# One stage for the modulation columns and the first projection of a two-block transformer layer

## The reference, cut to what matters

```
sh1, sc1, gt1, sh2, sc2, gt2 = split(silu(c) @ w_ada + b_ada, 6)              # w_ada is 2048 x 12288
csh1, csc1, ...              = split(silu(c_ctx) @ w_ada + b_ada, 6)
h  = rmsnorm(x,   norm1_g) * (1 + sc1)  + sh1
ch = rmsnorm(ctx, norm1_g) * (1 + csc1) + csh1
rq, rk, rv, rg, mq, mk, mv, mo, mg, gr, gm = split(h @ w_in)                  # and the same of ch
```

## Time and profile before

| | |
|---|---|
| median of three executions | 3499.36 us (3496.66 to 3500.38) |
| profiled execution, first to last instruction | 3498.0 us |
| mean granted TensorE clock | 0.914 of full speed |
| last matmul of phase 2 begins | 428.75 us |
| PE / PEld / DVE / ACT / POOL busy over the span | 84 / 59 / 53 / 33 / 68% |
| moved by DMA | 1015.86 MB, mean 290 GB/s |

### The profile page before, as it was taken

How to read it: one execution, slowest core, us unless ns; L and a number is a source line. 1 busy time by engine, 2 the same in 40 slices (tenths; PEclk the granted TensorE clock), 3 DMA queues, 4 the chain that set the end, 5 groups by cost and what they waited for, 6 DMA issues and landing times. The chain is left out here.

```text
span 3498.0 us, 31036 instructions
## 1 busy us (share of the span) xinstructions
PE 2928.4 (84%) x11330; PEld 2066.9 (59%) x11330; DVE 1862.3 (53%) x2379; ACT 1143.5 (33%) x1853; POOL 2390.3 (68%) x1133
## 2 busy tenths in 40 slices
PE   5899999999976666665456776569999999999999
PEld 1687778788853333322122232238888888888887
DVE  0767365532457787868888787761137421111121
ACT  2422354454421111111122112124445344444443
POOL 0444675688836676757677666758767688888887
PEclk9999999999988888877777887779999999999999
DMA  9899753455669999999999999986545455666554
GB/s 414 296 346 347 248 165 127 133 193 187 234 263 427 425 427 425 427 425 428 415 427 427 425 427 404 427 336 202 172 155 191 133 181 193 212 204 204 191 188 169
DMA packets 305995, 1015.86 MB, mean 290 GB/s; under 512 B 21916, under 2 KB 26616, under 8 KB 234928
## 3 DMA queue, kind: packets, MB, share of 16 engines
q1 hardware_dynamic: 228870, 472.46, 39.1%
q0 software_dynamic: 73728, 536.90, 36.4%
q10 hardware_dynamic: 3244, 4.51, 0.3%
HBM read 1009.58 MB, written 4.23 MB: 290 GB/s over the span
## 5 line engine op out<-in xcount | busy, mean ns | idle before, releaser
L670 POOL TENSOR_TENSOR block_weights_lo<-weight_ring,block_weights_hi 128x1024 fp32r<-128x1024 f32 x608 | 1483.6, 2449 | 611.1 <-ACT block_weights_hi L663 498.6
L1764 PE MATMUL banks<-up_rows,pick_diagonal 128*128 128x512 f32 x1024 | 675.4, 821 | 469.4 <-DMA up_rows<-peer_up,picked_experts 403.1
L663 ACT ACTIVATE block_weights_hi<-weight_ring 128x1024 fp32r<-128x1024 f32 x608 | 641.2, 1059 | 976.0 <-PE banks L2831 315.8
L1764 PEld LDWEIGHTS banks<-up_rows,pick_diagonal 128*128 128x128 f32 x1024 | 261.8, 268 | 852.2 <-issue 745.6
L1670 POOL DMA_INDIRECT up_rows<-peer_up,picked_experts x256 | 477.4, 1865 | 338.2 <-PE banks L1764 113.4
L2057 DVE CUSTOM_DVE_ANT_0 down_rows<-down_rows,h_tokens 128x2048 f32<-128x2048 f32 x256 | 584.3, 2290 | 203.2 <-DMA down_rows<-peer_down,picked_experts 198.3
L1662 POOL DMA_INDIRECT down_rows<-peer_down,picked_experts x256 | 422.3, 1649 | 116.2 <-issue 79.5
L2017 DVE SCALAR_TENSOR_TENSOR expert_sum<-up_rows,pick_share,expert_sum 128x2048 f32<-128x2048 f32 x125 | 293.9, 2351 | 57.9 <-ACT pick_share L1887 52.7
L1881 ACT ACTIVATE pick_gelu<-pick_dots 128x2 f32<-128x2 f32 x127 | 25.8, 203 | 828.1 <-DVE pick_dots L2057 828.0
L2264 PE MATMUL banks<-block_weights_hi,h_T_hi 128*128 128x512 f32 x704 | 282.2, 401 | 2.7 <-PEq L1534 2.7
L2266 PE MATMUL banks<-block_weights_hi,h_T_lo 128*128 128x512 f32 x704 | 275.2, 391 | 0.0
(11 more groups left out here) (500 smaller groups left out, 4412.2 us busy)
## 6 DMA issues: line engine op xcount, KB each, us to landing
weight_ring<-w_in SPq DMA_DIRECT2D x232, 1024.0 KB, 5.0
cond_ring<-w_ada SPq DMA_DIRECT2D x128, 512.0 KB, 6.1
weight_ring<-w_ada SPq DMA_DIRECT2D x32, 1024.0 KB, 8.6
weight_ring<-w_out SPq DMA_DIRECT2D x32, 1024.0 KB, 5.0
weight_ring<-peer_query SPq DMA_DIRECT2D x16, 1024.0 KB, 16.3
weight_ring<-w_ret_out SPq DMA_DIRECT2D x8, 1024.0 KB, 4.9
weight_ring<-w_mlstm_out SPq DMA_DIRECT2D x8, 1024.0 KB, 4.9
weight_ring<-w_mem_kv SPq DMA_DIRECT2D x8, 1024.0 KB, 16.4
```

What stands on the lines that cost most here:

```text
L663: act.activation(self.hi[:, self.place(slot, h)], ring.tile[:, slot, h * self.HALF:(h + 1) * self.HALF], ACT.Copy).then_inc(self.hi_ready, 1)
L670: pool.tensor_tensor(self.lo[:, at], ring.tile[:, slot, h * self.HALF:(h + 1) * self.HALF], self.hi[:, at], ALU.subtract).then_inc(ring.us ...
L1764: mm = pe.matmul(ps[:, 4 + b], diag[:, G % 2], up[:, p % ROWS, b * CG:(b + 1) * CG], start=(G % PER_TB == 0), stop=(G % PER_TB == PER_TB - ...
```

## The change

Both phases become one, `phase_opening`, with one set of semaphores and no barrier between them.

- SP issues `x` and `ctx` itself, before all else. The 32 tiles of `w_ada` now hold 128 rows of 1024 shift and 1024 scale columns. Tiles 0 to 15 (stage 0) give shift and scale of row blocks 0 to 7, tiles 16 to 31 (stage 1) those of row blocks 8 to 15. Behind each stage's tiles SP loads two tiles of `w_in`, so that the sequence has 36 entries, i = 0 to 35, over the four ring slots: 16 and 17 are `w_in` tiles 0 and 1, and 34 and 35 are tiles 2 and 3. The quarters are no longer begun before all 32 tiles are used.
- PE transposes two pairs of row blocks after each of `w_ada` tiles 4 to 7, instead of one row block after each of tiles 10 to 25. ACT copies the `x` part and DVE the `ctx` part, 512 columns at a time.
- After the first tile of stage 1, PE turns the columns of stage 0; ACT and DVE then modulate row blocks 0 to 7. From tile 20 on, PE runs one piece of the dense products of `w_in` tiles 0 and 1 after each tile of `w_ada`: 12 of their 16 pieces. The other 4 follow after the last tile.
- DVE does all modulation before its first quarter, and `QUARTERS` changes.
- Small tensors of phase 1 lie where the ring of the quarters will be.

The core of the diff (bodies that moved without a change of their instructions are left out):

```diff
-        QUARTERS = (8, 10, 10, 10, 10, 10, 6, 0)
+        QUARTERS = (2, 12, 12, 12, 11, 11, 4, 0)
+        STAGES, PAIRS = 2, KB // 2
+        STAGE_K, STAGE_W = KB // STAGES, SLOTS // STAGES
+        ADA_TILES = STAGES * KB
+        OPENING = STAGES * (KB + STAGE_W)
+        X_FROM, X_PER = 4, 2
+        PIECES_FROM = 4
+        is_weight = lambda i: i % (KB + STAGE_W) >= KB
+        weight_of = lambda i: i // (KB + STAGE_W) * STAGE_W + i % (KB + STAGE_W) - KB
+        base = ring.turn + OPENING // SLOTS - 1
         @block.sync
+            sp.dma_start(e.x[:], tokens_of(io["x"][0])).then_inc(x_in, 16)
+            sp.dma_start(raw, tokens_of(io["ctx"][0])).then_inc(ctx_in, 16)
+            for i in range(OPENING):
+                s, k = divmod(i, KB + STAGE_W)
+                before, slot = i - SLOTS, i % SLOTS
+                if before >= 0 and is_weight(before):
+                    sp.wait_ge(ring.used, base * SLOTS + weight_of(before) + 1)
+                elif before >= 0:
+                    sp.wait_ge(ada_used, ada_before(before) + 1)
+                if before >= 0:
+                    sp.sem_inc(ring.granted, 1)
+                if is_weight(i):
+                    sp.dma_start(ring.tile[:, slot], k_tile(w_in, weight_of(i), slice(RK, RK + CG))).then_inc(ring.landed[slot], 16)
+                else:
+                    rows = io["w_ada"][0][k * P:(k + 1) * P, 0:2 * D].rearrange("p (a n) -> p a n", a=2)
+                    sp.dma_start(ring.tile[:, slot].rearrange("p (a q) n -> p a (q n)", a=2), rows[:, :, s * 2 * CG:(s + 1) * 2 * CG]).then_inc(ada_landed[slot], 16)
+            sp.wait_ge(ada_used, ADA_TILES)
             for m in range(TILES):
...
         @block.scalar
...
+            for f in range(PAIRS):
+                act.wait_ge(x_turned, f + 1)
+                act.activation(e.hT[:, 2 * f:2 * f + 2].rearrange("p k t -> p (k t)"), ps[:, 4 + f % 2], ACT.Copy).then_inc(x_out, 1)
             act.dma_start(e.gate_bias[:], ...)
             act.dma_start(w_gate, ...)
+            act.wait_ge(ctx_turned_out, PAIRS)
...
             def modulate(first):
+                act.wait_ge(stage_ready, first // STAGE_K + 1)
                 for k in range(first, first + TILE_K, 2):
...
+            split.write_hi(act, ring, (0, base), 0)
             modulate(0)
             for m in range(TILES):
                 split.write_hi(act, ring, ((m + 1) % SLOTS, base + (m + 1) // SLOTS), m + 1)
                 if m + 1 < SLOTS:
                     modulate((m + 1) * TILE_K)
...
         @block.tensor
...
+            opening_pieces = [(m, h, j) for m in range(STAGE_W) for h in range(2) for j in range(2 * TB)]
+            for n in range(ADA_TILES):
+                s, k = divmod(n, KB)
+                ada_tile(s, k)
+                for f in range((n - X_FROM) * X_PER, (n - X_FROM + 1) * X_PER):
+                    if 0 <= f < PAIRS:
+                        if f == 0:
+                            pe.wait_ge(xn_ready, 4)
+                        turn_x(f)
+                if s and k == 0:
+                    turn_stage(s - 1)
+                p = n - KB - PIECES_FROM
+                if p >= 0:
+                    if p == 0:
+                        pe.wait_ge(x_out, PAIRS)
+                        pe.wait_ge(ctx_turned_out, PAIRS)
+                    dense_piece(*opening_pieces[p])
+            turn_stage(STAGES - 1)
+            for p in range(ADA_TILES - KB - PIECES_FROM, len(opening_pieces)):
+                dense_piece(*opening_pieces[p])
+
             for m in range(TILES):
-                dense(m)
+                if m >= STAGE_W:
+                    dense(m)
...
         @block.vector
...
+            for f in range(PAIRS):
+                dve.wait_ge(ctx_turned, f + 1)
+                dve.tensor_copy(e.chT[:, 2 * f:2 * f + 2].rearrange("p k t -> p (k t)"), ps[:, 2 + f % 2]).then_inc(ctx_turned_out, 1)
+            dve.wait_ge(x_out, PAIRS)
+            for s in range(STAGES):
+                dve.wait_ge(ada_used, (s + 1) * KB)
+                dve.tensor_copy(stage_rows[:, s % 2], bank_of(s)).then_inc(stage_out, 1)
+                dve.wait_ge(stage_turned, s + 1)
+                for a in range(2):
+                    step(dve.tensor_tensor(ada_of(s, a), turned_of(s, a), bias_of(s, a), ALU.add))
...
+                dve.wait_ge(stage_ready, s + 1)
+                for first in range(s * STAGE_K, (s + 1) * STAGE_K, TILE_K):
+                    for k in range(first + BY_SCALAR, first + TILE_K):
+                        sum_x(k)
+                    for k in range(first, first + TILE_K, 2):
+                        low_x(k)
+                        low_x(k + 1)
+                        low_ctx(k)
+                        low_ctx(k + 1)
+            for q in range(ADA2 * SLOTS):
```

More of the change, by code:

```diff
@@ L205, in gemm_token_major @@
             mm.then_inc(tb_done, 1)
[L208 to L334, removed]
-                tr.then_inc(cond_turned, 1)
-    ring.turn += ADA1
@@ L339, in phase_projection, with phase_opening @@
[L339 removed]
+def phase_opening(nc, e):
     ring, ps, io = e.ring, e.ps, e.io
@@ L353, in phase_projection @@
         w_gate_hi, w_gate_lo = w_gate_split[:, :, 0], w_gate_split[:, :, 1]
-        w_in, base = io["w_in"][0], ring.turn
+        w_in = io["w_in"][0]
+        cond_at = next_place(nc)
+        cond_tile = sb("cond_ring", [P, 4, TILE_K // 2, CG])
+        early = lambda name, shape, at: nc.alloc_sbuf_tensor_at(name, shape, F32, offset=cond_at + at)
+        raw, xn = e.cxt[:, :, 0:D], e.lat[:, 1, 0:TB * D].rearrange("p (b d) -> p b d", b=TB)
+        TILE_M = 32
+        rows_a, rows_b = early("rows_a", [P, P], 0), early("rows_b", [92, P], 512)
@@ new lines, in phase_opening @@
+        PIECES_FROM = 4
+        assert OPENING % SLOTS == 0 and 4 * TILE_M == P
+        is_weight = lambda i: i % (KB + STAGE_W) >= KB
+        weight_of = lambda i: i // (KB + STAGE_W) * STAGE_W + i % (KB + STAGE_W) - KB
+        ada_before = lambda i: sum(1 for n in range(i) if not is_weight(n))
+        base = ring.turn + OPENING // SLOTS - 1
+        ada_landed = [sem(f"ada_landed{s}") for s in range(SLOTS)]
+        ada_turn = lambda i: sum(1 for n in range(i % SLOTS, i + 1, SLOTS) if not is_weight(n))
@@ new lines, in phase_opening @@
+        assert ring.turn == 0 and all(i % SLOTS == weight_of(i) for i in range(OPENING) if is_weight(i))
+        bank_of = lambda s: ps[:, s % 2]
+        turned_of = lambda s, a: ps[:, 6 + s % 2].rearrange("p (i a q m) -> p a q i m", a=2, q=2, m=TILE_M)[:, a, :, :, 0:2]
+        ada_of = lambda s, a: e.ada[:, a * KB + s * STAGE_K:a * KB + (s + 1) * STAGE_K].rearrange("p (q i) v -> p q i v", q=2)
+        bias_of = lambda s, a: e.cols_a[:, a * KB + s * STAGE_K:a * KB + (s + 1) * STAGE_K].rearrange("p (q i) -> p q i", q=2).unsqueeze(3).to_broadcast([P, 2, TILE_K, 2])
@@ L503, in lhs, with dense_piece @@
                 return e.chT_hi[:, k, cols], e.chT_lo[k][:, cols]
+            def dense_piece(m, h, j):
+                c, t = divmod(m, SLOTS)
+                at, q = split.place(t, h), first_out[c] + j
+                if j == 0 and h == 0:
+                    pe.wait_ge(split.first_ready, m + 1)
+                elif j == 0:
+                    pe.wait_ge(ring.used, (base + c) * SLOTS + t + 1)
+                if c == 0 and j in (0, TB):
+                    pe.wait_ge(x_ready if j == 0 else ctx_ready, t * TILE_K + (h + 1) * split.HALF)
+                if t == 0 and h == 0 and q >= OUT_BANKS:
+                    pe.wait_ge(cols_out, q - OUT_BANKS + 1)
+                for kk in range(split.HALF):
+                    k = t * TILE_K + h * split.HALF + kk
+                    (hi, lo), w_hi, w_lo = lhs(k, j), split.hi[:, at, kk], split.lo[:, at, kk]
+                    pe.matmul(out_bank(q), hi, w_hi, start=(k == 0), stop=False, skip_group_check=True)
+                    pe.matmul(out_bank(q), hi, w_lo, start=False, stop=False, skip_group_check=True)
+                    mm = pe.matmul(out_bank(q), lo, w_hi, start=False, stop=(k == KB - 1), skip_group_check=True)
+                if j == width[c] - 1:
+                    mm.then_inc(split.free, 1)
+                elif t == SLOTS - 1 and h == 1:
+                    mm.then_inc(tb_done, 1)
@@ new lines, in dense, with ada_tile @@
+                    for j in range(width[m // SLOTS]):
+                        dense_piece(m, h, j)
+            def ada_tile(s, k):
+                i = s * (KB + STAGE_W) + k
+                pe.wait_ge(ada_landed[i % SLOTS], 16 * ada_turn(i))
+                for j in range(4):
+                    mm = pe.matmul(ps[j * TILE_M:(j + 1) * TILE_M, s % 2], cond_wide[:, k], ring.tile[:, i % SLOTS, j],
+                                   start=(k == 0), stop=(k == KB - 1), tile_position=(0, j * TILE_M))
+                mm.then_inc(ada_used, 1)
@@ new lines, in turn_x @@
+            def turn_x(f):
```

(25 more changed lines are left out.)

88 lines of the change are left out of this document (49 added, 39 removed).

## The result

The changed kernel takes 3513.2 us in the median of 5 executions, the kernel before 3500.4 us on the same chip: ratio 1.0038, interval 1.0027 to 1.005. I had forecast 3495.9 us and a range of 3485 to 3504. It is slower, and outside the range. The profiled span is 3508.2 us, 10.2 above the one of before.

A forecast was written before the change was run, and what follows sets the result against it. The read was taken to bound the opening up to 97 us, PE from 104.3. Twelve early pieces (16.3 us) against a stream start at 120.0 lowered 107.2 to 103.7; 3499.4 - 3.5 = 3495.9 us, range 3485 to 3504.

The forecast's parts named there:

- Tile 1's split stands behind `modulate(0)`: Turn into stage 1: ring slot 1 returns at 81.4 us, its tile lands at 86.3, reads idle about ten microseconds.
- first rival: Turn into stage 1: the slot comes back in time, i = 21 lands 10.5 us sooner, 3485.4 us; chance 0.22.
- 12 pieces hide: Stage 1: 12 dense pieces between tiles, 16.3 us of PE work, hide behind the read while the clock is up.
- the origin: Start of PE's dense stream, counted at full speed with 224 pieces: 107.2 us before, 103.7 after, 3.5 gained.
- tile 15's date: Stage 0's last `w_ada` tile lands at 56.8 us, bounds 52.4 to 60.
- term (3): Rest of stage 1: 12 tiles at 2.5 us, last landing 116.3; stream unbroken from 120.0 with 212 pieces left.
- 15 us at the last sum: Quarters: SP falling back 2 us per chunk costs nothing; last quarter done at 393 us, PE wants it at 408.
- 2.93 us per MB: Quarters' pace while SP lags behind PE: 85 MB at 2.93 us per tile before the last quarter's landing.
- The start of the quarters: DVE finishes modulation, with two quarters already in their ring, at about 141 us.
- the quarters become the bound: Rival: PE stands before its last sum if a tile costs more than 3.11 us; 3508 us at 3.25; chance 0.13.
- a bound of about 358 GB/s: Skill's HBM read limit per core: a tile never under 2.93 us, near 3515 us; 0.02 of the 0.13.
- the pieces hide nothing: Rival in stage 1: PE stays at 1.2 GHz, 12 steps cost some 20 us more, 3515 us; chance 0.03.

The follow-up runs named there:

- Experiment 3: Changed kernel, but ACT writes the high part of `w_in` tile 1 before `modulate(0)`: ratio 0.9994 to the kernel before, next phase at 428.71 us.
- experiment 6: experiment 1 with `PIECES_FROM` 16 instead of 4, so no dense pieces between stage 1's tiles: ratio 1.0051, next phase at 447.2 us.
- experiment 1: Changed kernel with `GATES_AT` 1 instead of 3, so DVE copies the gate rows before quarter 61, not 63: ratio 0.9997 to the kernel before.
- experiment 4: Changed kernel with both edits, gate rows copied earlier and `w_in` tile 1 split before the modulation: ratio 0.9972 to the kernel before.

## Why the prediction was wrong

**Right: the read's standstill.** "Tile 1's split stands behind `modulate(0)`" is what happened, by date too: slot 1 back at 82.6 (I had 81.4), the tile landed by 87.8 (86.3), a DMA rate of 1 GB/s between 72 and 83. Experiment 3 takes it away, for 11 us; my first rival had it at 10.5. That 12 pieces hide was right as well (experiment 6), and that PE, cold, begins stage 1 at 1.2 GHz.

**Off in size: the origin.** I had 103.7, measured 107.4. 1.7 us are tile 15's date (58.5 instead of 56.8), of which 1.5 are left at the tile of 87.8. The other 2.2 us lie in term (3), the rest of stage 1, and there in the step. From that tile to the third one's matmuls, cold, PE took 7.1 us; my terms imply about 7.0 (two reads of 2.5, and 2 of the "2 to 3 us behind"), so the cold start was right. But I took a later step as 2.36 us of PE work under a read of 2.5; it takes 2.60, at a granted clock of 1.00 and with PE busy throughout (95 to 121 us). The two changes between a tile's four matmuls and the dense ones cost most of the difference: 0.34 us instead of 0.23 behind the first dense matmul, and 0.32 instead of 0.23 ahead of the next tile. Over ten steps that is 2.3 us, and PE wins nothing back. So a gain of 3.5 us became none: that alone would have been "no difference", and experiment 1 shows exactly it.

**Wrong: "I cost it at nothing, and name its cover: 15 us at the last sum".** The last quarter was done at 412.8, where I had 393, and a wait that the sum does not have cost 11 us. Two things failed there. First the place. I looked for who waits for the quarters and found only the sums. The copy of the gate rows is queued among the quarters on DVE, and PE asks for it after m = 26, at 400.4, some 11 us ahead of the last sum (412.0 before). I had the constant in front of me and did not work out what it is relative to; 8.1 + 3 us hung on it. Second the pace. I took 2.93 us per MB from a stretch with 10 quarters in a chunk and used it for one with 12, where more of the bytes are quarters. In 127.4 us (loads m = 5 to 15 of the changed kernel) SP issued 60 transfers of quarters, 2.12 us each; in the 111.2 us of the earlier trace rows it was 54, 2.06 each. Counted by quarters both stretches agree, at 4.1 to 4.2 us; counted by MB they do not (3.18 and 2.93). A chunk with 12 then needs 50 us, not 46.9, and SP's lag became 26 us instead of the few I had. The start of the quarters was right (141.1), though not by its sum: 120.2 + 2 x 7.3 + 4 makes 138.8, not 141. So the 20 us lie in the pace alone, 3.16 us per MB over those 85.

The rival "the quarters become the bound" was thus the right mechanism, but I gave it 0.13 and put its place at the last sum, where PE did not wait in the changed kernel. That its 3508 us lie near the profiled span is luck: at the measured 3.16 its own sum puts the last quarter at 412.6, 4.6 late and not 12, and the 11 us came of another wait. What I had cited from the Trainium skill ("DMA: Bandwidth & Descriptors", section "Bandwidth"), a bound of about 358 GB/s, the changed kernel's trace does not show either: 408 GB/s over 35 us of stage 1. I had also read it too narrowly. The same section gives about 358 GB/s as what each of two cores gets when both stream, and 425 GB/s as measured for one core alone, and this program runs on one core. The rival "the pieces hide nothing" fell.

## What to carry to other kernels

When in-order work is shifted between stages, list every wait that another engine has on any instruction in that queue, the small copies with an index relative to the shifted work above all, and date each of them. Take the pace of a streamed operand from what its ring turns over (places, and the time of one round), not from the bytes that passed together with other loads. Where an early stage varies between executions, date each effect from a mark behind that stage. When loads of two uses share a ring in order, find for each slot which engine gives it back, and what stands ahead of that on the engine.

## What the runs showed of the hardware

A DVE operation of 128x16 elements between SBUF tiles, 0.17 us in the changed kernel (L623), took 2.15 us in experiments 3 and 4, where POOL was splitting a tile at the same time, and ended as POOL's pair did. In experiment 4:

```profile
66.22 4.66 POOL L699 TENSOR_TENSOR block_weights_lo<-weight_ring,block_weights_hi 128x1024 fp32r<-128x1024 f32 x2
...
68.76 2.15 DVE L625 SCALAR_TENSOR_TENSOR modulation_scale<-modulation_cols,cols_a 128x16 f32<-128x16 f32 x1
```

It delays the modulation by 2 us there, but it is not on the path, since the slot no longer waits for it. And the tiles of `w_ada` in runs of 4 KB came every 2.48 us at the end of experiment 6's stage 1, hardly slower than the 2.46 us of the 8 KB runs before, at the low end of my bounds.

The time at 1.2 GHz behind a wait of PE differed: 14 matmuls and 3.0 us lost after 8.1 us of idling in the changed kernel, 8 matmuls and 1.7 us lost after 7.7 us in experiment 3.
